# Starting the expert loop of a routed-expert layer five steps early, over the end of the output projection

## What is computed

```python
x = x + mix @ w_out[i]                       # output projection, (512,1024) @ (1024,1024)
h = rmsnorm(x, norm_ffn[i])
# router: top group of 4, then the top 2 of its 4 experts; combine holds the weights
for gi in range(N_GROUPS):                   # 16 experts in all, D_EXPERT = 512
    hid = silu(einsum('td,edf->etf', t, w_gate[sl])) * einsum('td,edf->etf', t, w_up[sl])
    hid = hid * combine[:, sl].T[:, :, None]
    out = out + einsum('etf,efd->td', hid, w_down[sl])
gate = sigmoid(rmsnorm(x, norm_ple[i]) @ w_ple_gate[i])
x = x + gate * (p[i] @ w_ple_proj[i])
return rmsnorm(x, norm_final)
```

## Time and profile before

| | |
|---|---|
| median of 3 runs | 645.91 us |
| the profiled execution: its time | 644.0 us |
| its span on the core | 642.2 us |
| TensorE busy | 578.1 us (90% of the span) |
| VectorE busy | 288.5 us (45%) |
| mean granted TensorE clock | 0.964 of full |
| moved by DMA | 151.52 MB, mean 236 GB/s |
| PE's instruction queue (q8) | 22 packets, 0.36 MB |

### The profile page before, as it was taken

One profiled execution on the slowest core, in us unless ns is written; L12 is line 12 of the kernel. 1 busy time (PEld: TensorE's weight loads), 2 busy tenths in 40 slices (PEclk: granted clock), 3 DMA queues, 4 the chain that ended last, 5 costly groups with the idle time before them and its releaser, 6 DMA issues.

```text
span 642.2 us, 9631 instructions
## 1 busy us (share of the span) xinstructions
PE 578.1 (90%) x3460; PEld 379.6 (59%) x3461; DVE 288.5 (45%) x627; ACT 186.8 (29%) x414; POOL 72.0 (11%) x111
## 2 busy tenths in 40 slices
PE   9999999999999999995489999997997776888994
PEld 8988877878989999995223223232232221235883
DVE  4521365456254333275135454543532333565753
ACT  5622255546443543331000000000000000343774
POOL 0000000000000000002113223232232222210000
PEclk9999999999999999989599999998997889989998
DMA  9852213212120159569278999999999999715001
GB/s 309 216 213 86 79 54 131 66 63 70 67 66 31 36 217 423 214 222 420 100 278 338 421 417 421 419 420 421 421 420 420 422 421 412 278 65 231 33 34 65
DMA packets 45586, 151.52 MB, mean 236 GB/s; under 512 B 8296, under 2 KB 27632, under 8 KB 35056
## 3 DMA queue, kind: packets, MB, share of 16 engines
q1 hardware_dynamic: 41520, 139.77, 55.5%
q0 software_dynamic: 3744, 11.02, 4.4%
q10 hardware_dynamic: 288, 0.27, 0.2%
HBM read 141.61 MB, written 9.45 MB: 235 GB/s over the span
## 4 chain that ended last, share of the span: by engine, by line
PE 70%; DMA 14%; DVE 7%; issue 4%; ACT 2%; SPq 2%; DVEq 0%
PE bank L1634 15%; DMA ring_gu<-in_w_up 13%; PE bank L1371 13%; PE bank L1373 12%; PE bank L1372 12%; PE bank L1654 8%; PE bank L1453 2%; PE bank L1426 2%; DVE ple_lo L1302 2%; SPq L590 1%; PE bank L1467 1%; DMA gmix<-in_norm_mix 1%; PE bank L1555 1%; PE bank L1436 1%; PE bank L1591 1%
## 5 line engine op out<-in xcount | busy, mean ns | idle before, releaser
L1634 PE MATMUL bank<-ring_gu,rowsT 128*64 128x512 f32 (+1 forms) x800 | 151.1, 623 | 25.5 <-DMA ring_gu<-in_w_up 21.1
L1634 PEld LDWEIGHTS bank<-ring_gu,rowsT 128*64 128x64 f32 (+1 forms) x800 | 45.9, 132 | 128.8 <-issue 102.4
L885 ACT ACTIVATE silu_g<-bank 128x256 f32<-128x256 f32 x20 | 7.7, 385 | 247.1 <-PE bank L1634 247.1
L1654 PE MATMUL bank<-ring_dn,hidT 128*64 128x512 f32 (+1 forms) x400 | 74.2, 604 | 4.5 <-DVE hidT L1256 4.2
L1275 DVE STREAM_TRANSPOSE rowsT<-rows 128x512 f32<-128x512 f32 x21 | 23.4, 1113 | 115.4 <-PE bank L1634 109.5
L1084 DVE TENSOR_TENSOR w_lo<-w_raw,w_hi 128x2048 fp32r<-128x2048 f32 x17 | 39.0, 2292 | 76.8 <-ACT w_hi L751 65.0
L1256 DVE STREAM_TRANSPOSE hidT<-hid 32x128 f32<-32x128 f32 x160 | 64.2, 402 | 1.9
L1371 PE MATMUL bank<-w_hi,hT_hi 128*128 128x256 f32 x192 | 55.4, 289 | 0.8 <-issue 0.6
L1373 PE MATMUL bank<-w_hi,hT_lo 128*128 128x256 f32 x192 | 54.3, 283 | 0.0
L1372 PE MATMUL bank<-w_lo,hT_hi 128*128 128x256 f32 x192 | 54.3, 283 | 0.0
L1654 PEld LDWEIGHTS bank<-ring_dn,hidT 128*64 128x64 f32 (+1 forms) x400 | 22.3, 128 | 54.1 <-issue 54.1
(11 more groups left out here) (218 smaller groups left out, 906.0 us busy)
## 6 DMA issues: line engine op xcount, KB each, us to landing
ring_gu<-in_w_gate SPq DMA_DIRECT2D x32, 1024.0 KB
ring_gu<-in_w_up SPq DMA_DIRECT2D x32, 1024.0 KB
ring_dn<-in_w_down SPq DMA_DIRECT2D x16, 2048.0 KB, 19.6
w_raw<-in_w_in SPq DMA_DIRECT2D x13, 1024.0 KB, 5.0
w_raw<-in_w_out SPq DMA_DIRECT2D x4, 1024.0 KB, 4.9
ple_gate_raw<-in_w_ple_gate SPq DMA_DIRECT2D x4, 1024.0 KB, 30.4
yg<-y_rows SPq DMA_DIRECT2D x8, 512.0 KB, 7.2
xr<-in_x SPq DMA_DIRECT2D x4, 512.0 KB, 8.8
```

The source lines that it names most:

```text
L1634: last = T.matmul(b_gu[q * BLK + t:q * BLK + t + n, :], rowsT[:, k, t:t + n], ring_gu[s][:, :, k, q * UC:(q + 1) * UC], start=(k == 0), st ...
L1654: last = T.matmul(b_dn[q * BLK + t:q * BLK + t + n, :], hidT[:, kf, t:t + n], ring_dn[s][:, kf, q * (D // 2):(q + 1) * (D // 2)], start=(k ...
```

## The change

TensorE now enters the loop after 11 of the 16 steps of the output projection. Six early turns (`EARLY`) come first: turns 0 to 4 each run one of the five remaining steps behind the two chains, turn 5 runs everything between the projection and the first block (`routed()`). A turn finds its piece by another chain of If/Else over the turn's number (`early_turn`). The first real block's gate/up product is in turn 6. As `total` isn't known when the loop begins, each turn reads `turn_limit` from SBUF, a large number until the router has written the true one.

Into the chains empty variants are put, "markers": numbers 6, 7 and 8 in that of gate/up (after variants 1, 3 and 5), 8 and 9 in that of down (after variants 3 and 7). Number 15 now skips a chain altogether by an If ahead of it. `EARLY_CODES` says how far each early turn walks: gate/up to marker 6 in turn 0, 7 in turn 1, 8 in turn 2; down to marker 8 in turn 3, 9 in turn 4. VectorE copies these codes to SBUF early on from the table of constants. Nothing is changed in the programs of SyncE, ScalarE and GpSimd.

```diff
-CODE_DN, CODE_GU_LOADS, CODE_DN_LOADS = 8, 128, 1024
-NO_GU, NO_DN = 2 * N_GU, 2 * N_DN
+CODE_DN, CODE_GU_LOADS, CODE_DN_LOADS = 16, 256, 2048
+GU_ORDER = [0, 1, 6, 2, 3, 7, 4, 5, 8]
+DN_ORDER = [0, 1, 2, 3, 8, 4, 5, 6, 7, 9]
+NONE = 15
+EARLY = 6
+EARLY_CODES = [(NONE, NONE), (6, NONE), (7, NONE), (8, 8), (NONE, 9), (NONE, NONE), (NONE, NONE)]
+TURNS = 32
...
+            dve.wait_ge(s_const, 16)
+            V.tensor_copy(step_code[:, 0:EARLY + 1], early_codes[0:1, 0:EARLY + 1]).then_inc(early_ready, 1)
+            V.tensor_copy(turn_limit[:], early_codes[0:1, EARLY + 1:EARLY + 2]).then_inc(early_ready, 1)
...
-            for m in range(NT * OUT_UNITS):
+            def out_step(m):
...
-            x1_transpose(NT * OUT_UNITS - 1)
-            logits(NT * OUT_UNITS - 2)
-            logits(NT * OUT_UNITS - 1)
+            for m in range(NT * OUT_UNITS - (EARLY - 1)):
+                out_step(m)
...
-            def one_of(products, number, n, pair=0):
+            def early_turn(turn, t=0):
 
-                with pe.If(number == pair):
-                    products((pair // 2, (pair + 1) // 2 % n))
-                if pair + 1 < 2 * n:
+                with pe.If(turn == t):
+                    if t < EARLY - 1:
+                        out_step(NT * OUT_UNITS - (EARLY - 1) + t)
+                    else:
+                        routed()
+                if t < EARLY - 1:
                     with pe.Else():
-                        one_of(products, number, n, pair + 1)
+                        early_turn(turn, t + 1)
+
+            def one_of(products, number, order, n):
+
+                with pe.If(number == order[0]):
+                    if order[0] < 2 * n:
+                        products((order[0] // 2, (order[0] + 1) // 2 % n))
+                if len(order) > 1:
+                    with pe.Else():
+                        one_of(products, number, order[1:], n)
...
-            with pe.Fori(0, MAX_BLOCKS + 2) as turn:
-                with pe.If(turn < total + 2):
-                    with pe.If(turn < total + 1):
-                        gate_up(turn, code_of(turn + 1))
-                    down(turn, code_of(turn))
-                    with pe.If(turn < 1):
-                        pe.wait_ge(table_ready, 1)
-                        kept_warm(8)
+            pe.wait_ge(early_ready, 2)
+            with pe.Fori(0, EARLY + MAX_BLOCKS + 1) as turn:
+                limit = pe.value_load(turn_limit[0:1, 0:1], min_val=EARLY + 1, max_val=EARLY + 1 + MAX_BLOCKS)
+                with pe.If(turn < limit):
+
+                    step = (turn + (TURNS + 1 - EARLY)) % TURNS
+                    with pe.If(turn + 1 < limit):
+                        gate_up(step, code_of(turn + 1))
+                    down(step, code_of(turn))
+                    with pe.If(turn < EARLY):
+                        early_turn(turn)
```

More of the change, by code:

```diff
@@ L260, in trunk @@
         (ident, tri, iota4, first_slots, grp_marks, ring_marks, minus_slot, pair_rows,
-         row_offset) = [small[:, a:a + w] for a, w in zip(starts, widths)]
+         row_offset, early_codes) = [small[:, a:a + w] for a, w in zip(starts, widths)]
         subln_b = at("subln_b", 98.25, [P, P])
@@ L310, in trunk @@
         cum_i = tiny("cum_i", [1, N_EXPERTS + 1], I32)
-        step_code = tiny("step_code", [1, 3 + MAX_BLOCKS], I32)
+        step_code = tiny("step_code", [1, EARLY + 2 + MAX_BLOCKS], I32)
+        turn_limit = tiny("turn_limit", [1, 1], I32)
         dqT = at("dqT", 124, [P, HEADS, SEQ])
@@ L1040, in route @@
                 V.tensor_scalar(cum_i[:, 0:N_EXPERTS], steps_r[:], -ROUND, None, ALU.add)
+                V.tensor_scalar(turn_limit[:], steps_r[:, N_EXPERTS - 1:], EARLY + 1 - ROUND, None, ALU.add)
                 link(V.tensor_scalar(cum_i[:, N_EXPERTS:], steps_r[:, N_EXPERTS - 1:], -ROUND - 1.0, None, ALU.add))
@@ L1580, in kept_warm @@
                     T.matmul(b_proj[2][:, 0:P], ones[:], ones[:], start=True, stop=True)
[L1582 to L1589, removed]
-                for n in range(2 * NT):
-                    last = T.matmul(b_rows[w],
-                                    slot_oh[:, n, :], blk_rows[:, w, n, :],
-                                    start=(n == 0), stop=(n == 2 * NT - 1))
-                last.then_inc(rows_done, 1)
@@ L1618, in column_tiles, with gate_up @@
                 return [(q, g * GRP, GRP, slots[g]) for g in range(2) for q in range(2)]
-            def gate_up(turn, code):
+            def gate_up(step, code):
                 loads = code // CODE_GU_LOADS % (CODE_DN_LOADS // CODE_GU_LOADS)
                 def products(slots):
-                    pe.wait_ge(xT_ready, turn)
-                    pe.wait_ge(hid_ready, turn)
+                    pe.wait_ge(xT_ready, step)
+                    pe.wait_ge(hid_ready, step)
                     for k in range(KD):
@@ L1639, in products, with down @@
                     last.then_inc(gu_done, 1)
-                one_of(products, code % CODE_DN, N_GU)
-            def down(turn, code):
+                number = code % CODE_DN
+                with pe.If(number < NONE):
+                    one_of(products, number, GU_ORDER, N_GU)
+            def down(step, code):
                 loads = code // CODE_DN_LOADS
                 def products(slots):
-                    pe.wait_ge(hidT_ready, turn)
-                    pe.wait_ge(y_ready, turn)
+                    pe.wait_ge(hidT_ready, step)
+                    pe.wait_ge(y_ready, step)
                     pe.wait_ge(s_dn[slots[0]], 16 * loads + 16)
```

48 lines of the change are left out of this document (35 added, 13 removed).

## The result

The changed kernel takes **683.95 us** (median of 4 runs, 681.63 to 684.87) against 645.81 us before: ratio 1.0589, with a 95% interval of 1.0554 to 1.0624. Forecast were 683.6 us and a range of 655 to 712. The profiled execution spans 683.0 us, before 642.2. In experiments 1 and 2 one run each came out over 1.5% slower than the other three, and the medians given there are of those three. That the sum came out says nothing yet about its terms, so each is read by itself.

A forecast was written before the change was run, and what follows sets the result against it. Bound by 15.5 us of TensorE code fetch before the experts, then by DMA loads. 644.0 + 25.4 + 13.4 + 4 + 4 - 9.1 = 681.7, plus 1.9 for the median, 683.6 us; range 655 to 712.

The forecast's parts named there:

- Part 1: Before the first expert product: code resident, so the stall goes, 10.9 us less 1.8 for the clock, gain 9.1 us.
- Parts 2 and 3: In the projection's end: early turns' chain walks idle TensorE 25.4 us; turn 0's three jumps fetch code for 13.4 us.
- the cover: In the early turns: work still in TensorE's queue hides 2.0 us of each walk, 6 x 2.0 in all.
- Part 4: At the projection's end: gaps may put the clock at its lower level, costing 4 us, between 0 and 8.
- Part 5: In the later turns: one more read and two more tests each, mostly covered by DMA, 4 us, between 1 and 10.
- The sum: Whole kernel: all terms added to the profiled 644.0 give 681.7 us; 1.9 more for the median gives 683.6 us.
- A: Rival on the loop's code: it no longer fits and blocks are fetched again each turn, about 740 us; chance 0.10.
- B: Rival in the projection: the sequencer runs far enough ahead that walks and fetches hide beside matmuls, 638 us; chance 0.05.
- C: Rival on the markers: they bring nothing, blocks come again or late and part of the stall stays, 698 us; chance 0.10.

The follow-up runs named there:

- experiment 1: The changed kernel with all early codes NONE, so turns 1 to 4 leave both chains at once: 672.20 us, ratio 1.0419.
- experiment 2: The changed kernel with a single early turn, turn 0 doing steps 11 to 15 and the router's part: 653.33 us, ratio 1.0147.
- experiment 4: The kernel before with one more register read in each loop turn (the number of turns, from cum_i): 650.46 us, ratio 1.0080.
- experiment 5: The changed kernel with all early codes NONE and EARLY = 8, seven projection steps in the loop in place of five: 825.1 us, ratio 1.2783.
- experiment 6: The kernel before with an added turn 0 split over the router's two waits, no limit read in a turn: 639.29 us, ratio 0.9919.
- experiment 9: Kernel before with turn 0 split over the router's waits, plus 6 MB of loads held until the slot sums' first half: 636.04 us, ratio 0.9875.
- experiment 10: Kernel before with turn 0 split over the router's waits, plus 6 MB of loads held until block tables are written: 640.88 us, ratio 0.9951.
- experiment 3: The changed kernel with the loop begun behind the whole projection, EARLY = 1, last transposes and logits ahead of it: 654.19 us, ratio 1.0134.
- experiment 8: The kernel before with one SyncE line holding 6 MB of expert loads until the slot sums' first half is done: 649.84 us, ratio 1.0090.
- experiment 7: Kernel before with turn 0 split over the router's waits, plus gate/up code kept in a register for the down product: 638.68 us, ratio 0.9913.

## Why the prediction was right, step by step

- **Part 1, the stall that goes (9.1 us forecast, 12.6 measured).** The mechanism is as described; the size left its range (7.5 to 10.9). I took 1.8 us off for the first product at the lower clock. It ran in 7.09 us against 7.97 in the earlier trace rows, as the dummies now last until shortly before it. The lower clock took its share elsewhere: the slot sums ran in 5.44 us against 3.78. And "what is late next is the gather, which DMA at full load holds back" was read from before alone. After the change the last gather is issued at 345.30 and `rowsT` starts at 349.20; before, 299.37 and 305.85: 2.6 us less, with a DMA share of 0.54 over 345:350 where it was 1.03 over 299.3:305.5.
- **Parts 2 and 3, walks and fetches (25.4 + 13.4 = 38.8 us forecast, 33.9 of gaps measured).** The sequencer's own time was forecast closely. From leaving one step to reaching the next it took 14.0, 9.6, 7.0, 6.5, 7.8 and 5.7 us in turns 0 to 5, 50.6 together, against 37.4 + 13.4 = 50.8. The fetches in it were 5.2, 4.1 and 3.3 us for the 6.2, 3.6 and 3.6 forecast. The 3.6 came from a row read as "DMA nearly idle"; the share was 0.22 over 310:313.7, and 0.56 over the longer stretch of the earlier trace rows. The term mis-sized is the cover: 50.6 - 33.9 = 16.7 us, not 12.0. I took 2.0 us a turn, measured at full clock; at the lower clock the same queue holds more work. Ahead of step 13 the sequencer left step 12 at 289.8 and TensorE ended it at 293.0, 3.2 us later. The gaps ahead of steps 13 to 15 and of the transposes follow the walk as foretold, 3.93, 3.21, 5.63 and 2.18 us for 12, 9, 15 and 7 branches. The 7.03 ahead of step 12 is outside the foretold 2 to 6, because the third jump stands there.
- **The Trainium skill's figure for a branch.** By about 108 ns (Advanced Engine Details and Errata, Control Flow Timing, of the Trainium skill) 28 branches would have given 3.0 us in experiment 1; the gaps shrank by 7.1. The rows' 0.27 us, from the start of one taken branch to the start of the next, stands.
- **Part 4, the clock (4 us net).** Steps 11 to 15 took 5.4, 5.9, 6.1, 5.0 and 6.4 us in place of 3.55, 11.0 us more. Some 4.9 of it, the difference of the forecast 38.8 and the 33.9 of gaps, comes back as cover. With the 0.7 by which step 10 ends after the start that step 11 had before, that is 6.8 net, inside 0 to 8. Check: 33.9 + 11.0 + 0.7 = 45.6, the lateness of step 15.
- **Part 5, the later turns (4 us forecast, 7.8 measured).** Inside the range, 1 to 10. That DMA's limit covers the longer turns was right: the lateness of 44.5 us, where no turn had yet waited for a load, fell to 34.9 in those that did before. The turns up to the end of the last expert product added 4.2 us, 1.1 of it by that product itself (6.44 us against 5.35, at the lower clock). What failed is that the sum has no term behind the last block: the empty turns there now read too. 3.6 us came there, 2.2 of them standing; experiment 4 shows the same place.
- **The sum.** Parts 2 to 4 came out 2.8 us higher, part 5 3.8, part 1 3.5 the other way: 3.1 us in the profiled execution (684.9 against 681.7). The 1.9 us added for the median hid it, since the median of the four runs lies 0.9 under the profiled one and not above. That 683.6 met 683.95 so closely is luck of signs; that it was slower by 38 us is not.
- **Rivals.** A did not happen, but with eight blocks touched or asked for and eight that fit nothing was to spare: experiment 5 showed its mechanism two steps further on, at a greater price than I gave it. The Trainium skill (Runtime: NRT & Kernel Launch, Instruction fetch mechanics) gives PE 128 KiB in blocks of 16 KiB, which makes eight, and this trace and experiment 5 agree. Its second rule, that a taken branch out of a window of two blocks forces a fetch, is contradicted by every kernel here that kept five to eight blocks over the expert turns. B fell with the first gap of 11.96 us. C was half right: the markers bring nothing (experiment 1), but turn 0's jumps bring it all, and no packet starts after 281.5, as turn 1 begins.

Open is which block the ninth displaces, and whether the change's eighth is needed or only asked for ahead. No kernel with exactly one step more in the loop was run.

## What to carry to other kernels

A branching loop's code is fetched when it is first walked, and that first walk should lie where its engine waits for another one anyway, with the DMA queues held quiet: the fetch and the walk around it left TensorE standing for 15.5 us before, for 12 to 20 us in the change and in six of the experiments, for 5.8 in experiment 6 and not at all in experiments 9 and 10. Moving loop iterations into a stretch where the engine is busy pays the walk each time: count reads and taken branches per turn against what the engine's queue holds. A loop with a fixed number of turns pays them in its empty turns too, where no work is left to hide them. Before code is pulled into a loop, count its blocks, since one too many costs far more than any stall that is saved.

## What the runs showed of the hardware that I had not expected

- Eight blocks of code stay, and with a ninth they are fetched again, nine packets a turn (experiment 5): a cliff, some 153 us for two more steps in the loop.
- A jump into a block that isn't there takes 3.3 to 3.4 us with a DMA share of 0.02 (the change's third jump, the second of experiment 9), 3.9 at 0.68 and 4.4 at 0.76 (the first jumps of experiments 9 and 6), and 4.9 to 6.5 with DMA full (experiments 3, 6 and 8). Where it brings the skipped block too, it takes 4.1 at 0.03 (the change's second). Bulk loads issued by one engine slow down another one's branches where these have to fetch.
- A register read of 0.75 us costs 5.7 us when one is added to each turn and gives nothing measurable when one is taken away from each turn that has work (experiments 4 and 7). More than half of the cost arises in the turns that do nothing.
